# Value pages of the sampled sequences: key pages first, five buffers, the last value products inside the attention loop

## The chip, the cores and the metric

The kernel runs on one core of one Trainium2 chip. The metric is the device time of one execution in microseconds, the median over several executions. The core has five engines: TensorE (PE, matrix products), VectorE (DVE), ScalarE (ACT), GpSimd (POOL) and SyncE (SP), which here only issues transfers. ACT issues some transfers too, and POOL a few. All engines run their own instruction streams and meet at semaphores.

## What is computed

The reference is one inference step of a two-layer decoder for a prompt of 512 tokens and for 8 sampled sequences with one new token each. The even layer joins attention with a forgetting gate (8 heads of 64) and a convolution; the odd layer is a retention layer; each has a gated feed-forward part. The change touches the attention of the 8 sampled sequences over their paged past (1024 tokens, 8 pages of 128 tokens each, found through a page table):

```python
kp = cache_k[e, page_table].reshape(Bd, -1, H, hd)
vp = cache_v[e, page_table].reshape(Bd, -1, H, hd)
s_p = einsum('bqhd,bkhd->bhqk', q, kp) * scale
s_p = s_p + cq[..., None] - cum_p.transpose(0, 2, 1)[:, :, None, :]
p = softmax(concatenate([s_p, s_n], axis=-1), axis=-1)
o = einsum('bhqk,bkhd->bqhd', p[..., :P], vp) + einsum('bhqk,bkhd->bqhd', p[..., P:], v)
```

So 64 key pages and 64 value pages of 256 KB each are read, all of them once.

## The kernel before

The order of the work is written out by hand. After the input projection of the even layer comes the **attention loop**: 32 steps x = 0 to 31, a step for each of 8 heads and 4 blocks of 128 prompt queries. In each step PE transposes the weights of that step (line 715 in the rows), makes the scores of step x + 6 (L995 to L998) and, in every fourth step, a head's output (`head_out`, L1007). DVE finds the row maxima, ACT takes the exponentials and copies banks out, POOL divides by the row sums (L2443). The work of the sampled sequences, of the convolution and of the output projection is hung into the steps by tables at the top of the file (`V_AT`, `GATHER_AT`, `V_LOAD_AT`, `CONV_OUT_AT` and others).

**Key pages.** SP loads the 64 key pages into a ring of four buffers `kp`; page g may be loaded once POOL has made the product of page g - 4 (`key_pages`). POOL multiplies each page with a sequence's query row held in `QB` (three pages in a step, L2466), DVE sums the products (`dots`, L2019). POOL's stream is in order: the divisions and the products wait for one another.

**Value pages.** A *unit* u is four value pages; sequence b has the units 2b and 2b + 1. SP loads pages 0 to 2 of a unit and ACT page 3 (`values` and `V_LOAD_AT`), each through `value_unit` (from L619), which first waits until the buffer is free. Before the change the buffer is u modulo 3: `vp_a`, `vp_b`, `vp_c`. PE multiplies a sequence's eight pages with its weights (`past_values`, L1074, eight matmuls for each unit), ACT copies the bank into `vm`, which is the first two rows of `QB`, and PE picks each head's part out of it (`gather`, L1084), which DVE adds to `full_s` (L2081). The weights of sequences 0 to 3 are ready at step 16, those of 4 to 7 at step 26 (`DN_AT`).

Before, the value products of sequences 0 to 6 stand in steps 17, 19, 21, 23, 27, 29, 31. Those of sequence 7 and the gathers of 6 and 7 stand behind the loop (L1154 to L1156). SP's stream is in order too, and units 3 and 4 stand in it between key page 55 and key page 56.

**Output projection.** Its convolution half (`conv_out`, 24 matmuls each, line 827 in the rows) runs beside the loop in steps 19, 20, 22, 24, 25, 26, 28, 30, each with a weight block that ACT and DVE split into a high and a low part (`w_hi` L1360, `w_lo` L1802). Its attention half (`run("out_even", ...)`) runs behind the loop and starts with the gathered rows of the sampled sequences (`G_hi`, `G_lo`). PE fills steps up to 17 with idle products (L1121).

Of the kernel before, what the change touches and what calls it, by code (L numbers as in the profile page):

```python
# [17 lines left out]
D = 1024  # L18
# [3 lines left out]
NB = 8  # L22
# [6 lines left out]
NPG = NB * PAGES  # L29
# [62 lines left out]
EXP_AT = {15: 0, 25: 1}  # L92
DN_AT = {16: 0, 26: 1}

V_AT = {17: 0, 19: 1, 21: 2, 23: 3, 27: 4, 29: 5, 31: 6}
GATHER_AT = {18: 0, 20: 1, 22: 2, 24: 3, 28: 4, 30: 5}
V_LOAD_AT = {9: ((2, (0, 1)),), 10: ((2, (2, 3)),), 18: ((3, (3,)), (4, (3,))), 20: ((5, (3,)), (6, (3,))),
             22: ((7, (3,)), (8, (3,))), 24: ((9, (3,)), (10, (3,))), 28: ((11, (3,)), (12, (3,))),
             30: ((13, (3,)), (14, (3,)))}

PER_STEP = 3
STEP_PRODUCTS = 3
# [78 lines left out]
def psum_jobs():  # L181


    jobs = [(("xT", k), "D") for k in range(KD)] + [("xs", "D")]
# [22 lines left out]
    for h in range(HEADS):  # L207
        for q in range(TB):
# [25 lines left out]
            if x in DN_AT:  # L234
                jobs += [(("dn", DN_AT[x]), "D")]
            if x in GATHER_AT:
                jobs += [(("og", GATHER_AT[x]), "D")]
            if x in V_AT:
                jobs += [(("ov", V_AT[x]), "A")]
    jobs += [(("og", NB - 2), "D"), (("ov", NB - 1), "A"), (("og", NB - 1), "D")]  # L240
    for g in range(ADA_EVEN, ADA_LATE, 2):
        jobs += norm(1) if g == ADA_EVEN else norm(2) if g == ADA_NORM else []
        jobs += [(("adr", g), "A"), (("adr", g + 1), "A"), (("ada", g), "D"), (("ada", g + 1), "D")]
# [84 lines left out]
def build(nc, A):  # L328
# [3 lines left out]
    jobs = Jobs()  # L332
# [4 lines left out]
    def sb(name, shape, dtype=f32):  # L337
        t = nc.alloc_sbuf_tensor_at(name, shape, dtype, offset=at[0])
        at[0] += (math.prod(shape[1:]) * 4 + 31) // 32 * 32
        assert at[0] <= nc.sbuf_usable_end, (name, at[0])  # L340
        return t
# [90 lines left out]
    QB = sb("QB", [P, NB, 512])  # L432
# [13 lines left out]
    kp = sb("kp", [P, 4, 512])  # L446
# [11 lines left out]
    vp_c = sb("vp_c", [P, 4, 512])  # L458
    at[0] = ring_at
    vp_a = sb("vp_a", [P, 4, 2, 512])  # L460
    vp_b = sb("vp_b", [P, 4, 2, 512])
# [82 lines left out]
    with ctx:  # L544
        def sem(name):
            return ctx.enter_context(nc.semaphore(name))
# [6 lines left out]
        x_loaded, rows_loaded, pages_loaded = sem("x_loaded"), sem("rows_loaded"), sem("pages_loaded")  # L553
        raw_loaded = [sem(f"raw_loaded{i}") for i in range(4)]
        k_page = [sem(f"k_page{i}") for i in range(4)]
        v_unit = [sem(f"v_unit{i}") for i in range(3)]
        early_loaded = [sem(f"early_loaded{i}") for i in range(4)]
        spare_loaded = [sem(f"spare_loaded{i}") for i in range(4)]
        late_loaded = [sem(f"late_loaded{i}") for i in range(4)]
# [7 lines left out]
        sq_used, v_used = sem("sq_used"), sem("v_used")  # L567
# [23 lines left out]
        pad_ready, p_ready, prod_ready = sem("pad_ready"), sem("p_ready"), sem("prod_ready")  # L591
# [10 lines left out]
        cache_v = A["cache_v"][0].rearrange("n p h d -> n p (h d)")  # L602

        def page(eng, g, cache, dst, arrived):

            n = eng.value_load(pt_row[0:1, ds(g, 1)], min_val=0, max_val=cache.shape[0] - 1)
            eng.dma_start(dst, cache[ds(n, 1), :, :].rearrange("o p n -> p (o n)")).then_inc(arrived, 16)
# [6 lines left out]
            return (prod_a, prod_b)[g % 4 // 2][:, g % 2, :]  # L614

        def value_page(u, j):
            return vp_c[:, j] if u % 3 == 2 else (vp_a, vp_b)[u % 3][:, j, 1]

        def value_unit(eng, u, js):  # L619

            if u < 2:
                eng.wait_ge(block_done, N_OUT_EVEN)
                eng.wait_ge(lo_ready, N_OUT_EVEN)
            elif u == 2:
                wait_job(eng, ("cq", 1))
            elif u % 2 == 0:
                wait_job(eng, ("ov", (u - 3) // 2))
            else:
                eng.wait_ge(v_used, (u - 3) // 2 + 1)
            for j in js:  # L630
                page(eng, 4 * u + j, cache_v, value_page(u, j), v_unit[u % 3])

        def wait_job(eng, name):

            eng.wait_ge(job_done, jobs.done(name))
# [66 lines left out]
        def _(pe):  # L702
            def open_job(name):

                i = jobs.index[name]
                if i >= 4:
                    pe.wait_ge(emptied[jobs.engine[i - 4]], jobs.nth[i - 4])
                return Jp[i % 4]

            def close(mm):  # L710
                mm.then_inc(job_done, 1)
# [356 lines left out]
            def past_values(b):  # L1068
                bank = open_job(("ov", b))
                pe.wait_ge(samp_dve, 7 + 5 * (b // 4))  # L1070
                for u in (2 * b, 2 * b + 1):
                    pe.wait_ge(v_unit[u % 3], 64 * (u // 3 + 1))
                    for j in range(4):
                        mm = pe.matmul(bank[QD * j:QD * j + QD, :], weights_of(b, u % 2 * 4 + j), value_page(u, j),  # L1074
                                       start=u % 2 == 0, stop=u % 2 == 1)
                    if u % 2 == 0:
                        mm.then_inc(v_used, 1)
                close(mm)

            def gather(b):  # L1080
                bank = open_job(("og", b))
                wait_emptied(pe, ("ov", b))
                for t in range(4):
                    mm = pe.matmul(bank[:, 2 * t:2 * t + 2], vm[:, b % 2, t * P:(t + 1) * P],  # L1084
                                   con[:, C_OWN + 2 * t:C_OWN + 2 * t + 2], start=True, stop=True)
                close(mm)
# [23 lines left out]
            for h in range(HEADS):  # L1110
                for q in range(TB):
# [34 lines left out]
                    if x in DN_AT:  # L1146
                        past_total(DN_AT[x])
                    if x in GATHER_AT:
                        gather(GATHER_AT[x])
                    if x in V_AT:  # L1150
                        past_values(V_AT[x])
                    if x in CONV_OUT_AT:
                        conv_out(CONV_OUT_AT[x])
            gather(NB - 2)  # L1154
            past_values(NB - 1)
            gather(NB - 1)  # L1156

            pe.wait_ge(g_ready, 5)
# [197 lines left out]
        def _(act):  # L1356
# [112 lines left out]
            for m in range(20):  # L1469
# [22 lines left out]
                if m < 8 and m % 2 == 1:  # L1492
                    j = m // 2
# [5 lines left out]
                else:  # L1499
                    kind, j = m // 4, m % 4  # L1500
# [65 lines left out]
            def past_values(b):  # L1566
                wait_job(act, ("ov", b))
                if b >= 2:
                    wait_job(act, ("og", b - 2))
                n.up(f(vm[:, b % 2, :], Jp[jobs.bank(("ov", b))][:, :], ACT.Copy), emptied["A"])  # L1570
# [9 lines left out]
            for h in range(HEADS):  # L1580
# [3 lines left out]
                for q in range(TB):  # L1584
# [26 lines left out]
                    if x in EXP_AT:  # L1611
                        past_exps(EXP_AT[x])
                    if x in V_AT:
                        past_values(V_AT[x])
                    if x == SILU_AT:
# [6 lines left out]
                    if x in CONV_OUT_AT:  # L1622
                        ahead(N_OUT_EVEN + CONV_OUT_AT[x] + 2)
                    for u, js in V_LOAD_AT.get(x, ()):
                        if u == 2:
                            act.wait_ge(pages_loaded, 32)
                        value_unit(act, u, js)
            value_unit(act, 2 * NB - 1, (3,))
            past_values(NB - 1)

            def gates(layer):

# [149 lines left out]
        def _(dve):  # L1782
# [294 lines left out]
            def gather(b):  # L2077
                bank = bank_of(("og", b))
                for e in range(2):
                    r = slice(HD * e, HD * e + HD)  # L2080
                    o = v.tensor_tensor(full_s[r, 0:4, b], full_s[r, 0:4, b],  # L2081
                                        bank[r, 0:8].rearrange("p (t e) -> p t e", e=2)[:, :, e], ALU.add)
                n.up(o, emptied["D"])
# [26 lines left out]
            for h in range(HEADS):  # L2110
                for q in range(TB):
# [24 lines left out]
                    if x in DN_AT:  # L2136
                        past_scale(DN_AT[x])
                    if x in GATHER_AT:
                        gather(GATHER_AT[x])
                    for t in CONV_HI_AT.get(x - 1, ()):  # L2140
# [5 lines left out]
                    if x in CONV_OUT_AT:  # L2146
                        i = CONV_OUT_AT[x]
                        lo(N_OUT_EVEN + i + 2)
                        update(i, N_OUT_EVEN + i, mod_at(0, 2))
            gather(NB - 2)  # L2150
            gather(NB - 1)
            n.own(emptied["D"])
            step(v.tensor_copy(G_hi[:, 0:4, 0:NB], full_s[:, 0:4, :]))
# [374 lines left out]
        def _(sp):  # L2528
# [56 lines left out]
            def key_pages(first, end):  # L2585

                if first == 0:
                    for j in range(4):
                        page(sp, j, cache_k, kp[:, j], k_page[j])
                    return  # L2590
                with sp.Fori(first // 4, end // 4) as i:
                    for j in range(4):
                        sp.wait_ge(prod_ready, 4 * i + j - 3)
                        page(sp, 4 * i + j, cache_k, kp[:, j], k_page[j])

            def out_weights(first, end):

                for n in range(first, end):
                    half = 1 if n < N_OUT_EVEN + KD else 0
                    load_n(n, A["w_out_even"][0], 4 * half, P * ((n - N_OUT_EVEN) % KD), 4)  # L2600

            def values(first, end):
                for u in range(first, end):
                    value_unit(sp, u, (0, 1, 2, 3) if u < 2 else (0, 1, 2))

            N = N_OUT_EVEN
            key_pages(0, 4)
            out_weights(N, N + 4)
            values(0, 2)
            key_pages(4, 56)  # L2610
            values(3, 5)
            key_pages(56, 64)
            out_weights(N + 4, N + 6)
            values(5, 7)
            out_weights(N + 6, N + 7)
            values(7, 9)
            out_weights(N + 7, N + 9)
            values(9, 11)
            out_weights(N + 9, N + 11)
            values(11, 13)  # L2620
            out_weights(N + 11, N + 12)
            values(13, 16)
            out_weights(N + 12, N + 16)

            def ffn(layer):
                wg, wu, wd = A["w_ffn_gate"][layer], A["w_ffn_up"][layer], A["w_ffn_down"][layer]
# [102 lines left out]
```

## Time and profile before

| | us |
|---|---|
| median of 3 executions | 1847.53 |
| fastest and slowest of them | 1842.29, 1848.11 |
| the profiled execution, its own time | 1839.13 |
| span of its records, first to last instruction | 1837.3 |
| PE busy in the span | 1740.0 |
| DVE, ACT, POOL busy | 873.3, 579.0, 216.3 |

All times of the rows are microseconds from the start of the span. The attention loop's scores begin at 205.9 and its last head output ends at 384.1; the attention half of the output projection starts at 397.48. A busy engine in the profile is one that executes something, at whatever speed; the granted clock of PE stands in a column of its own (1.00 is full, 0.50 is half).

### The profile page before, as it was taken

What the parts mean: (1) busy time and instruction counts of PE and PEld (TensorE: products, weight loads), DVE (VectorE), ACT (ScalarE), POOL (GpSimd) and SP (SyncE); (2) the same over time, 40 slices, a digit from 0 to 9 for tenths busy, and PEclk for the clock granted to TensorE, in tenths of its full rate; (3) what the DMA queues carried; (4) which work ended last, traced back from release to release, by engine and by line L of the source; (5) the groups of instructions that cost most, each with busy time, mean ns of one, the idle gap of its engine ahead of it and who ended that gap; (6) DMA issues with size and microseconds to landing.
All of it is one profiled execution on the core that took longest, in us unless ns stands there. A gap on an engine that the chain in (4) does not pass through costs nothing.

```text
span 1837.3 us, 32367 instructions
## 1 busy us (share of the span) xinstructions
PE 1740.0 (95%) x13122; PEld 1556.5 (85%) x13122; DVE 873.3 (48%) x1529; ACT 579.0 (32%) x847; POOL 216.3 (12%) x229
## 2 busy tenths in 40 slices
PE   5899998988999999999999999999998999999998
PEld 3889754666999999998978888798687999999998
DVE  3599666626223233235417546365475533333335
ACT  2332344314321222223324434334323432222223
POOL 1000386202000000001001102001111000000001
PEclk7899998988999999999999999999999999999999
DMA  8554565674344535422324616237642233233321
GB/s 299 157 174 152 167 205 173 201 249 162 88 135 131 170 91 184 161 72 78 109 70 121 206 58 202 84 105 218 218 155 87 58 92 104 81 91 93 92 72 56
DMA packets 288329, 248.92 MB, mean 135 GB/s; under 512 B 9256, under 2 KB 240072, under 8 KB 288207
## 3 DMA queue, kind: packets, MB, share of 16 engines
q1 hardware_dynamic: 265156, 177.91, 32.1%
q0 software_dynamic: 15824, 58.99, 9.3%
q10 hardware_dynamic: 7235, 10.42, 1.7%
q8 instruction: 81, 1.33, 0.3%
q14 instruction: 33, 0.27, 0.1%
HBM read 224.05 MB, written 23.70 MB: 135 GB/s over the span
## 4 chain that ended last, share of the span: by engine, by line
PE 83%; DVE 6%; POOL 3%; ACT 3%; issue 3%; DMA 1%; ACTq 1%; SPq 0%; POOLq 0%; DVEq 0%
PE product L827 62%; PE product L842 5%; PE job L1327 2%; POOL sqa L2435 2%; PE job L721 2%; PE job L1310 1%; PE job L751 1%; PE job L715 1%; PE job L1302 1%; PE job L1201 1%; PE job L1221 1%; PE job L794 1%; PE job L1007 1%; DVE rstd L1832 1%; PE job L995 1%
## 5 line engine op out<-in xcount | busy, mean ns | idle before, releaser
L827 PE MATMUL product<-H_hi,w_lo 128*128 128x260 f32 x2368 | 676.4, 286 | 4.0 <-ACT gate L1360 3.7
L827 PE MATMUL product<-H_lo,w_hi 128*128 128x260 f32 x2368 | 671.0, 283 | 0.0
L827 PE MATMUL product<-H_hi,w_hi 128*128 128x260 f32 x2368 | 670.3, 283 | 0.0
L827 PEld LDWEIGHTS product<-H_hi,w_lo 128*128 128x128 f32 x2368 | 447.7, 189 | 17.4 <-issue 14.1
L827 PEld LDWEIGHTS product<-H_hi,w_hi 128*128 128x128 f32 x2368 | 448.4, 189 | 0.0
L827 PEld LDWEIGHTS product<-H_lo,w_hi 128*128 128x128 f32 x2368 | 448.0, 189 | 0.2
L1802 DVE TENSOR_TENSOR w_lo<-raw,w_hi 128x1024 fp32r<-128x1024 f32 (+2 forms) x244 | 279.8, 1147 | 160.0 <-ACT w_hi L1360 158.8
L1360 ACT ACTIVATE w_hi<-raw 128x1024 fp32r<-128x1024 f32 (+2 forms) x244 | 237.9, 982 | 209.6 <-PE product L827 155.9
L827 PE MATMUL product<-G_hi,w_lo 128*128 128x260 f32 x912 | 260.7, 286 | 6.1 <-DVE X L1887 2.5
L827 PE MATMUL product<-G_lo,w_hi 128*128 128x260 f32 x912 | 259.2, 284 | 0.0
L827 PE MATMUL product<-G_hi,w_hi 128*128 128x260 f32 x912 | 258.4, 283 | 0.0
L2187 DVE TENSOR_TENSOR full<-gate,product 128x520 f32<-128x520 f32 x44 | 30.7, 697 | 334.6 <-PE product L827 330.1
L827 PEld LDWEIGHTS product<-G_hi,w_lo 128*128 128x128 f32 x912 | 173.0, 190 | 11.6 <-issue 11.5
L827 PEld LDWEIGHTS product<-G_hi,w_hi 128*128 128x128 f32 x912 | 173.1, 190 | 0.0
L827 PEld LDWEIGHTS product<-G_lo,w_hi 128*128 128x128 f32 x912 | 172.9, 190 | 0.0
L1884 DVE TENSOR_TENSOR upd_s<-product,mod 128x8 f32<-128x8 f32 x80 | 13.3, 166 | 195.9 <-PE product L827 149.8
L1360 ACT ACTIVATE G_hi<-full 128x520 f32 (+1 forms) x44 | 28.2, 640 | 208.7 <-DVE full L2187 208.6
L1924 DVE SCALAR_TENSOR_TENSOR CV<-UP,vec,CV 128x512 f32<-128x512 f32 x120 | 80.9, 743 | 0.1
L1360 ACT ACTIVATE gate<-product 128x520 f32<-128x520 f32 x48 | 29.0, 605 | 156.2 <-PE product L827 156.1
L2435 POOL TENSOR_TENSOR sqa<-sq 128x520 f32<-128x520 f32 x5 | 6.5, 1298 | 559.6 <-ACT sq L1360 559.6
L2471 POOL DMA_DIRECT2D spare<-in_ada_w x24 | 18.0, 758 | 340.3 <-PE job L721 304.3
L842 PE MATMUL product<-G_hi,w_lo 128*128 128x260 f32 x176 | 50.2, 285 | 3.6 <-DVE w_lo L1802 3.6
(343 smaller groups left out, 2192.8 us busy)
## 6 DMA issues: line engine op xcount, KB each, us to landing
spare<-in_ada_w POOLq DMA_DIRECT2D x24, 1024.0 KB, 9.7
raw<-in_w_in_odd SPq DMA_DIRECT2D x48, 512.0 KB, 3.8
raw<-in_w_ffn_gate SPq DMA_DIRECT2D x44, 512.0 KB, 4.0
raw<-in_w_ffn_up SPq DMA_DIRECT2D x44, 512.0 KB, 3.7
kp<-in_cache_k SPq DMA_DIRECT2D x64, 256.0 KB, 2.9
raw<-in_w_ffn_down SPq DMA_DIRECT2D x32, 512.0 KB, 4.2
st<-in_state_ret POOLq DMA_DIRECT2D x28, 512.0 KB, 4.3
out_ret_sample<-st POOLq DMA_DIRECT2D x28, 512.0 KB, 4.8
```

The costliest lines, as they stand in the source:

```text
L715: return pe.transpose(out, src, ident[0:n, 0:n])
L721: mm = pe.matmul(bank[QD * q:QD * q + QD, :], cT[:, 4 * half + q, :], weights[:, q, :], start=half == 0, stop=half == 1)
L751: mm = pe.matmul(bank[:, j * 10:(j + 1) * 10], ada_rows(g)[:, j * P:(j + 1) * P], con[:, C_ALL:C_ALL + 10], start=True, stop=True)
L794: return pe.matmul(banks[c][:, 0:CH], con[:, C_MEAN:C_MEAN + 1].broadcast_to((P, P)), src[:, c * CH:(c + 1) * CH], **kw)
L827: mm = pe.matmul(Gp[slot][:, c, 0:CH], w[:, j, k, :], x[:, (first + k) % KD, cols], start=k == 0 and p == 0, stop=k == kt - 1 and p == 2)
L842: mm = pe.matmul(Gp[j][:, c, 0:CH], w[:, j, k, :], x[:, k, c * CH:(c + 1) * CH], start=k == 0 and p == 0, stop=k == kt - 1 and p == 2)
L1327: mm = pe.matmul(bank[:, j * P:L], RVN[:, j, e * P:(e + 1) * P], AD[:, j, 0:L - j * P], start=j == 0, stop=j == TB - 1)
L1360: return nc.scalar.activation(out, in_, func, **kw)
L1802: v.tensor_tensor(w_lo[:, j, 0:kt, :], raw[:, j, 0:kt, :], w_hi[:, j, 0:kt, :].bitcast(f32), ALU.subtract).then_inc(lo_ready, 1)
L1924: o = v.scalar_tensor_tensor(CV[:, t, NB:T], UP[:, t, w:w + L], cw, CV[:, t, NB:T], ALU.mult, ALU.add)
L2187: v.tensor_tensor(dst.rearrange("p (c n) -> p c n", c=2), up.rearrange("p (c n) -> p c n", c=2), Gp[1][:, :, 0:CH], ALU.mult).then_inc(slo ...
L2435: n.up(v.tensor_tensor(sqa[:], a, sq[:, k % 2, :], ALU.add), sq_used)
```

## The change

Six things change, and nothing else:

1. SP loads the key pages 4 to 63 in one go; units 3 and 4 come behind key page 63, not between pages 55 and 56.
2. The value products move: sequences 0 to 7 in steps 17, 20, 22, 24, 27, 28, 30, 31 (before 17, 19, 21, 23, 27, 29, 31 and behind the loop); the gathers of 0 to 6 in steps 19, 21, 23, 25, 28, 30, 31 (before 0 to 5 in 18, 20, 22, 24, 28, 30). Only the gather of sequence 7 stays behind the loop.
3. Units 11 and 13 get buffers of their own: the key ring `kp`, and rows 2 to 5 of `QB`, both free once all 64 key products are made. Units 12, 14 and 15 go to `vp_c`, `vp_a` and `vp_b`.
4. ACT issues page 3 of units 3 and 4 in step 18, of 5 and 6 in step 21, of 7 and 8 in step 23, of 9, 10, 11 and 13 in step 25, of 12 and 14 in step 28, of 15 in step 29.
5. SP's order behind it: units 9, 10, 11, 13, then two blocks of output weights, then 12, 14, 15, then the other five blocks.
6. The waits before a unit's loads follow the new buffers.

```diff
-V_AT = {17: 0, 19: 1, 21: 2, 23: 3, 27: 4, 29: 5, 31: 6}
-GATHER_AT = {18: 0, 20: 1, 22: 2, 24: 3, 28: 4, 30: 5}
-V_LOAD_AT = {9: ((2, (0, 1)),), 10: ((2, (2, 3)),), 18: ((3, (3,)), (4, (3,))), 20: ((5, (3,)), (6, (3,))),
-             22: ((7, (3,)), (8, (3,))), 24: ((9, (3,)), (10, (3,))), 28: ((11, (3,)), (12, (3,))),
-             30: ((13, (3,)), (14, (3,)))}
+V_AT = {17: 0, 20: 1, 22: 2, 24: 3, 27: 4, 28: 5, 30: 6, 31: 7}
+GATHER_AT = {19: 0, 21: 1, 23: 2, 25: 3, 28: 4, 30: 5, 31: 6}
+V_LOAD_AT = {9: ((2, (0, 1)),), 10: ((2, (2, 3)),), 18: ((3, (3,)), (4, (3,))), 21: ((5, (3,)), (6, (3,))),
+             23: ((7, (3,)), (8, (3,))), 25: ((9, (3,)), (10, (3,)), (11, (3,)), (13, (3,))),
+             28: ((12, (3,)), (14, (3,))), 29: ((15, (3,)),)}
+LATE_SLOT = {11: 3, 12: 2, 13: 4, 14: 0, 15: 1}
+def value_slot(u):
+    return LATE_SLOT.get(u, u % 3)
+def value_loads(u):
+    return sum(value_slot(i) == value_slot(u) for i in range(u + 1))
...
-    jobs += [(("og", NB - 2), "D"), (("ov", NB - 1), "A"), (("og", NB - 1), "D")]
+    jobs += [(("og", NB - 1), "D")]
...
         def value_page(u, j):
-            return vp_c[:, j] if u % 3 == 2 else (vp_a, vp_b)[u % 3][:, j, 1]
+            s = value_slot(u)
+            return (vp_a[:, j, 1], vp_b[:, j, 1], vp_c[:, j], kp[:, j], QB[:, 2 + j])[s]
...
             elif u == 2:
                 wait_job(eng, ("cq", 1))
+            elif u in (11, 13):
+                eng.wait_ge(prod_ready, NPG)
+            elif u == 12:
+                eng.wait_ge(v_used, 5)
+            elif u == 14:
+                wait_job(eng, ("ov", 4))
+            elif u == 15:
+                eng.wait_ge(v_used, 6)
             elif u % 2 == 0:
                 wait_job(eng, ("ov", (u - 3) // 2))
             else:
                 eng.wait_ge(v_used, (u - 3) // 2 + 1)
...
-            gather(NB - 2)
-            past_values(NB - 1)
             gather(NB - 1)
...
-            value_unit(act, 2 * NB - 1, (3,))
-            past_values(NB - 1)
...
-            key_pages(4, 56)
+            key_pages(4, 64)
             values(3, 5)
-            key_pages(56, 64)
             out_weights(N + 4, N + 6)
             values(5, 7)
             out_weights(N + 6, N + 7)
             values(7, 9)
             out_weights(N + 7, N + 9)
-            values(9, 11)
+            values(9, 12)
+            values(13, 14)
             out_weights(N + 9, N + 11)
-            values(11, 13)
-            out_weights(N + 11, N + 12)
-            values(13, 16)
-            out_weights(N + 12, N + 16)
+            values(12, 13)
+            values(14, 16)
+            out_weights(N + 11, N + 16)
```

## Rows read from the trace of the kernel before

**Rows 1.** The page: busy time of PE, and the chain that ended last, by engine.
```profile
PE 1740.0 (95%) x13122; PEld 1556.5 (85%) x13122; DVE 873.3 (48%) x1529; ACT 579.0 (32%) x847; POOL 216.3 (12%) x229
...
PE 83%; DVE 6%; POOL 3%; ACT 3%; issue 3%; DMA 1%; ACTq 1%; SPq 0%; POOLq 0%; DVEq 0%
```

**Rows 2.** Timeline of POOL: start, length, instruction, idle time before it and its releaser.
```profile
304.28 3.01 POOL L2466 TENSOR_TENSOR prod_b<-kp,QB 128x512 f32<-128x512 f32 x2
318.16 1.26 POOL L2466 TENSOR_TENSOR prod_a<-kp,QB 128x512 f32<-128x512 f32 x1 [10.87 <-DMA kp<-in_cache_k]
```

**Rows 3.** Timeline of SP's transfers, steps 17 to 20.
```profile
307.67 2.53 SPq L607 DMA_DIRECT2D vp_a<-in_cache_v  x3
310.97 2.53 SPq L607 DMA_DIRECT2D vp_b<-in_cache_v  x3
314.89 11.03 SPq L607 DMA_DIRECT2D kp<-in_cache_k  x8
```

**Rows 4.** Timeline of DVE, steps 18 and 19.
```profile
309.30 1.26 DVE L2019 TENSOR_REDUCE SC<-prod_b 128x8 f32<-128x512 f32 x2
319.45 0.69 DVE L2019 TENSOR_REDUCE SC<-prod_a 128x8 f32<-128x512 f32 x1 [8.89 <-POOL prod_a L2466]
...
320.41 3.19 DVE L1806 TENSOR_TENSOR G_lo<-CV,G_hi 128x520 fp32r<-128x520 f32 x2
323.52 2.38 DVE L1802 TENSOR_TENSOR w_lo<-raw,w_hi 128x512 fp32r<-128x512 f32 x2
```

**Rows 5.** Timeline of PE, steps 18 to 20: a gather, a head, value products, a transpose.
```profile
308.83 1.00 PE L1084 MATMUL job<-con,QB 128*128 128x2 f32 x8
...
312.93 4.03 PE L1007 MATMUL job<-PTS,VN 128*64 128x512 f32 x8 [1.61 <-ACT PTS L1360]
320.44 1.94 PE L1074 MATMUL job<-vp_c,SC 128*32 128x512 f32 x8 [3.47 <-DVE full_s L2081]
...
328.35 0.28 PE L715 MATMUL job<-con,SS_a 128*128 128x128 f32 x1
```

**Rows 6.** Busy time by stretch, then granted clock, DMA share, GB/s.
```profile
300.00:306.00 6.00, 6.00 (x14) 2.84 (x18) 4.41 (x9) 3.75 (x8) 2.92 (x4) 0.50 0.16 43
313.00:316.00 3.00, 3.00 (x5) 1.00 (x6) 0.00 (x0) 0.00 (x0) 0.00 (x0) 0.54 0.93 305
392.00:402.00 10.00, 8.04 (x37) 6.31 (x30) 1.30 (x5) 1.63 (x3) 3.12 (x4) 0.50 0.35 124
```

**Rows 7.** The chain that ended last, steps 20 and 21: start, length, what.
```profile
331.12 0.48 DVE nm L2008
...
332.41 4.35 DMA vp_c<-in_cache_v
...
336.81 1.10 PE job L1074 x8
...
340.01 2.99 PE product L827 x24
```

**Rows 8.** Value pages issued by ACT, 300 to 400 us: time from issue to landing.
```profile
DMA to landing us min/median/max: 3.7/4.1/4.4
```

**Rows 9.** Timeline of ACT: the page transfer that follows the one at 332.41.
```profile
333.48 0.35 ACTq L607 DMA_DIRECT2D vp_a<-in_cache_v  x1
```

**Rows 10.** The chain that ended last, step 31 and behind the loop.
```profile
381.75 2.34 PE job L1007 x8
384.09 1.07 PE job L1074 x8
...
388.09 3.61 DMA vp_a<-in_cache_v
...
393.75 0.60 ACT QB L1360
...
394.50 1.85 PE job L1084 x8
...
397.48 2.53 PE product L827 x10
```

More of the change, by code:

```diff
@@ L555, in build @@
         k_page = [sem(f"k_page{i}") for i in range(4)]
-        v_unit = [sem(f"v_unit{i}") for i in range(3)]
+        v_unit = [sem(f"v_unit{i}") for i in range(5)]
         early_loaded = [sem(f"early_loaded{i}") for i in range(4)]
@@ L630, in value_unit @@
             for j in js:
-                page(eng, 4 * u + j, cache_v, value_page(u, j), v_unit[u % 3])
+                page(eng, 4 * u + j, cache_v, value_page(u, j), v_unit[value_slot(u)])
         def wait_job(eng, name):
@@ L1071, in past_values @@
                 for u in (2 * b, 2 * b + 1):
-                    pe.wait_ge(v_unit[u % 3], 64 * (u // 3 + 1))
+                    pe.wait_ge(v_unit[value_slot(u)], 64 * value_loads(u))
                     for j in range(4):
@@ L2149, in _ @@
                         update(i, N_OUT_EVEN + i, mod_at(0, 2))
-            gather(NB - 2)
             gather(NB - 1)
```

## The prediction

> **What bounds the kernel now.** I read the page first. PE is busy for 1740 of 1837.3 us and holds 83% of the chain that ended last [rows 1], so only time that PE loses, or runs at half clock, can be won. Of the attention stage I then read the timelines of POOL, SP, DVE and PE, and the chain. Two places lose time.
>
> The first is a hole at steps 18 and 19. POOL finishes the product of key page 55 at 307.3 and stands idle for 10.87 us until page 56 lands [rows 2]. SP could not issue it: units 3 and 4 stand in front, unit 4 waits until sequence 0's products are done, and so the eight last key pages go out only from 314.89 [rows 3]. DVE needs page 56's product in step 18 and stands idle for 8.89 us at 319.45; behind it in its stream are the last two splits of the convolution (3.19) and the first two weight splits (2.38) [rows 4]. PE's value products of sequence 1 therefore start only at 320.44, 3.47 idle before them, and step 20 begins at 328.35 [rows 5].
>
> The second is the end of the loop. The last head is done at 384.09; then come sequence 6's products, a page that lands only at 391.7 (issue 388.09 and 3.61), sequence 7's products, a copy and a gather, and the output projection starts at 397.48 [rows 10]: 13.4 us. PE's clock has dropped to half by then (0.50 from 392 to 402 [rows 6]).
>
> **The change part by part.** I follow PE, in the span's time, from 316.96, where head 4 ends (312.93 and 4.03 [rows 5]). That head waits for ACT's copy of step 19's transposes, which doesn't move, so I keep it.
>
> *Key pages ahead.* Page 56 waits for products made long before, so it is there when POOL wants it at 307.3. DVE sums it at 310.56, directly behind 309.30 and 1.26, and its weight splits end at 325.90 - 8.89 = 317.0 [rows 4]. PE has sequence 0's gather behind the head now (1.00 [rows 5], moved from step 18), so it reaches the first `conv_out` at 318.0: PE is last, not DVE. With 2.99 for the block [rows 7], step 20 starts at 320.9 and not at 328.35: 7.4 earlier, but with sequence 1's products still to do.
>
> *Units 3 and 4 behind page 63.* Page 63 needs the product of page 59. POOL makes four products from 307.3 on, at 1.26 each [rows 2] with a division between, so about 313.9; unit 3 goes out by 318 and lands, at the 4.1 of a page [rows 8], at 322. PE reaches its second unit of sequence 1 at about 323. No wait, but a microsecond of cover only.
>
> *Products moved into the loop.* From 328.35 to 384.09 PE took 55.7 us with sequences 2 to 5 in it; now 1 to 6 lie there, two more, at two units of 1.10 each [rows 7]: +4.4. Gathers 1 to 5 lie there both times.
>
> *New waits at ACT's pages.* Before, ACT issued page 3 of unit 5 in step 20, behind that step's row maximum; from the maximum to the product it took 336.81 - 331.12 = 5.7 us, and a `conv_out` block of 2.99 on PE covered half of it [rows 7]. Now it issues in step 21, where no block follows. PE has only a gather, step 22's transposes and scores (together 340.01 - 337.91 = 2.1 [rows 7]) and the first unit (1.10): a wait of 5.7 - 3.2 = 2.5 in step 22. Unit 7's page is issued behind head 5 in step 23: about 0.8 for the issue (331.60 to 332.41) and 4.1 to land [rows 7, 8] against a gather, transposes, scores and a unit, some 3.9 (an estimate from the 2.1 and 1.10 above, with wider scores): a wait of 1.0 in step 24. Bounds for both together: zero if the pages land in time, 8.2 if each waits a whole landing. I take 3.5, because the rows for issue and landing are of the same instructions under the same load. The Trainium skill ("DMA: Bandwidth & Descriptors", section "Anatomy of one DMA") gives some 2.0 us fixed plus bytes over 436 GB/s, fitted on the software path; for 256 KB that is an estimate of 2.6, and the two waits would be 1.0 and 0. This trace has 4.1, and the measurement decides.
>
> *The other loads.* ACT issues four pages in step 25, 4 x 1.07 on its queue (332.41 to 333.48 is one [rows 7, 9]), with step 26's copy behind them; a `conv_out` block and a transpose cover that. If the cover were gone it would cost 4.3, less what PE still has to do. Units 9 to 15 go out one to three steps before use: nothing. The output weights behind unit 15 are the same number and wait for the same splits: nothing; without that cover, one landing of about 4.
>
> So head 7 ends at 320.9 + 55.7 + 4.4 + 3.5 = 384.5, 0.4 later than before: the loop's own win is spent on two more sequences.
>
> *The tail.* Behind head 7 stand sequence 6's gather (1.0), sequence 7's products (2.2), the copy (393.75 to 394.50, 0.8), the last gather at full clock (1.0, before 1.85) and 1.13 to the first product [rows 10]: 6.1, against 13.4. The projection starts at 390.6 instead of 397.48: 6.9 earlier.
>
> *The clock.* Before, the projection's first 4.4 us ran at half [rows 6]. With idle pieces of 0.8 and 1.1 only, shorter than the 1.61 in front of the drop at 313 [rows 5, 6], I expect full clock: -2.2. In return the wait of 2.5 in step 22 is longer than that 1.61, so I add one drop there, at the price of a head at either level, 4.03 - 2.34 = 1.7 [rows 5, 10]. Bounds of the clock terms: -2.2 to +3.4.
>
> **Sum:** -6.9 - 2.2 + 1.7 = -7.4 us. Everything behind is PE's chain and shifts as a whole. Against the profiled execution this is 1839.13 - 7.4 = 1831.7. That execution was 8.4 faster than the median shown, and the runs shown spread over 5.8; I subtract from the median: 1847.53 - 7.4 = 1840.1.
>
> **The rivals.**
> - *Full win.* The pages of steps 22 and 24 land in time and no clock drops there: -7.4 - 3.5 - 1.7 = -12.6, 1834.9. For it: if PE comes to step 22 later than I have it, each microsecond takes one off the wait, and the clock then stays up. Against it: no page of ACT's landed under 3.7 [rows 8]. Chance 0.22.
> - *Half a win.* The tail's clock drops as before, and step 24's wait drops it a second time: -7.4 + 2.2 + 1.7 = -3.5, 1844.0. For it: at 392 to 402 PE was busy for 8.04 of 10 us and still at 0.50, and in 300 to 306 busy throughout [rows 6]. Chance 0.22. Beside it, a rule of the Trainium skill ("TensorE: Matmul & The Clock Gate", section "HAM oscillation"): short compute between waits for transfers makes the clock fall at every such wait, which speaks against moving these products close behind their pages. In this trace the clock did fall at 313 behind a wait of 1.61, though that one was for ACT.
> - *Slower: each unit waits for its pages.* Place: steps 20, 22, 24 and 30, where pages are issued a step ahead. If each waits a whole landing (4.1) and drops the clock (1.7), that is 23.2 in place of the 5.2 in the sum: -7.4 + 18.0 = +10.6, 1858.1. It is slower by over 0.3% once waits and drops exceed 5.2 + 7.4 + 5.5 = 18.1. For it: unit 3 has a microsecond of cover. Against it: sequences 4 to 7 have their pages 5 us or more ahead. Chance 0.06.
> - *The hole stays.* POOL or DVE is held at step 18 by something else, and 7 us of hole stay: about -0.4, 1847.1. Against it: at 307.3 POOL waits for the page alone [rows 2]. Chance 0.05.
>
> **How the numbers follow.** My forecast has 0.45. A measurement of this kernel tells about 0.3%, 5.5 us, from no change. Faster by more: 0.45 x 0.9 for the forecast, 0.22 for the full win, a quarter of the half win: 0.68. Within 0.3%: 0.25. Slower: 0.07. The range reaches from the full win, with 3 us for the level of the runs, to the half win with 2: 1832 to 1846. It leaves out the last two rivals and some of the edges.
>
> **What would show it.** Right: POOL's idle time at page 56 is gone; step 20's first transpose comes about 7 us earlier; step 22 has a wait of some 2.5 us on `vp_c`; step 31's head ends near 384; behind it no wait for a page, and the projection starts near 390 at full clock. Wrong: head 7 ending much before 382 (the waits were overstated) or after 387; a new idle piece of POOL or DVE over 3 us in steps 18 to 24; PE at half clock behind 390; or a part behind the loop whose length changes.

## The result, and the profile after

| | before | changed |
|---|---|---|
| first comparison, median (runs) | 1842.29 (9) | 1832.56 (9) |
| fastest and slowest | 1838.85, 1848.11 | 1826.19, 1841.09 |
| ratio, 95% interval | | 0.9938 [0.9918, 0.9957] |
| the profiled execution, its span, mean granted clock | 1839.13, 1837.3, 0.975 | 1835.99, 1834.2, 0.971 |

The change is faster: by 9.7 us between the medians, by 11.4 (8 to 15) by the ratio. The forecast was 1840.1 and -7.4: right in sign, inside its range (1832 to 1846), 7.5 us too high. The changed kernel ran twice more beside the kernel before: ratios 0.9959 [0.9942, 0.9976] and 0.9940 [0.9920, 0.9961]. The mean of all 28 runs is 1834.0, that of 80 runs of the kernel before 1844.1: 10.1 us (standard error 1.0).

The two profiled executions differ by only 3 us, because one ran longer at half clock. The windows of the changed kernel, then of the one before (PE only: stretch, its length, PE's busy time and instructions, granted clock, DMA share, GB/s):

```profile
272.00:283.00 11.00, 10.46 (x44) 0.84 0.68 212
283.00:304.00 21.00, 21.00 (x60) 0.52 0.41 114
304.00:320.00 16.00, 12.33 (x63) 1.00 0.41 121
340.00:352.00 12.00, 9.94 (x49) 0.57 0.81 247
402.00:412.00 10.00, 10.00 (x73) 0.83 0.97 358
```

```profile
283.00:304.00 21.00, 18.47 (x82) 0.89 0.55 159
```

In steps that the change does not touch, PE was busy for all of 283 to 304 and had a clock of 0.52; before, the same stretch had 0.89. Everything behind stands some 8.4 us later in the record of the changed kernel for this reason (step 18's first transpose at 316.08, before at 307.66), so the rows below are compared by distances from that transpose.

**The hole at step 18 is closed.** POOL's timeline, then DVE's (start, length, instruction, idle before it and its releaser), to be held against [rows 2, 4]:

```profile
313.99 0.59 POOL L2460 TENSOR_SCALAR SS_b<-SS_b,ri 128x384 f32<-128x384 f32 x1 [1.78 <-DVE ri L2030]
314.54 3.01 POOL L2483 TENSOR_TENSOR prod_b<-kp,QB 128x512 f32<-128x512 f32 x2
317.51 1.73 POOL L2483 TENSOR_TENSOR prod_a<-kp,QB 128x512 f32<-128x512 f32 x1
```

```profile
318.30 1.25 DVE L2037 TENSOR_REDUCE SC<-prod_b 128x8 f32<-128x512 f32 x2
319.48 0.67 DVE L2037 TENSOR_REDUCE SC<-prod_a 128x8 f32<-128x512 f32 x1
320.07 3.32 DVE L1824 TENSOR_TENSOR G_lo<-CV,G_hi 128x520 fp32r<-128x520 f32 x2
323.31 2.38 DVE L1820 TENSOR_TENSOR w_lo<-raw,w_hi 128x512 fp32r<-128x512 f32 x2
```

Neither the 10.87 before page 56's product nor the 8.89 before its sum is left: both follow directly. SP's timeline shows the price, unit 3 behind the last key page:

```profile
305.92 19.78 SPq L620 DMA_DIRECT2D kp<-in_cache_k  x10
326.64 2.53 SPq L620 DMA_DIRECT2D vp_a<-in_cache_v  x3
329.95 2.54 SPq L620 DMA_DIRECT2D vp_b<-in_cache_v  x3
```

PE's timeline, steps 18 to 22 and from head 7 to the projection (see [rows 5, 10]):

```profile
316.08 0.55 PE L737 MATMUL job<-con,SS_a 128*128 128x128 f32 x3
...
321.93 4.50 PE L1029 MATMUL job<-PTS,VN 128*64 128x512 f32 x8 [3.06 <-ACT PTS L1380]
326.36 1.43 PE L1106 MATMUL job<-con,QB 128*128 128x2 f32 x8
...
330.60 0.27 PE L737 MATMUL job<-con,SS_a 128*128 128x128 f32 x1
...
332.07 1.10 PE L1096 MATMUL job<-vp_c,SC 128*32 128x512 f32 x8
332.98 1.05 PE L1096 MATMUL job<-vp_a,SC 128*32 128x512 f32 x8
...
340.79 1.94 PE L1096 MATMUL job<-vp_b,SC 128*32 128x512 f32 x8
344.79 1.95 PE L1096 MATMUL job<-vp_c,SC 128*32 128x512 f32 x8 [2.06 <-DMA vp_c<-in_cache_v]
...
392.80 2.34 PE L1029 MATMUL job<-PTS,VN 128*64 128x512 f32 x8 [0.78 <-ACT PTS L1380]
...
396.05 1.10 PE L1096 MATMUL job<-vp_a,SC 128*32 128x512 f32 x8
396.96 1.04 PE L1096 MATMUL job<-vp_b,SC 128*32 128x512 f32 x8
398.81 1.02 PE L1106 MATMUL job<-con,QB 128*128 128x2 f32 x8 [0.81 <-ACT QB L1380]
400.98 0.38 PE L849 MATMUL product<-G_hi,w_lo 128*128 128x260 f32 x1 [1.15 <-DVE G_lo L1824]
```

Step 20 begins 14.5 us behind step 18, before 20.7 (17.4 and 13.1 in the other two profiles of the changed kernel, 23.0 in the second of the kernel before). Sequence 1's products have no wait. Sequence 2's second unit, in step 22, has one of 2.06, and the two units there take nearly twice their time (1.94 and 1.95 against 1.10 and 1.05). The last step's head ends at 395.13 and the projection follows 5.85 us later, before 13.4; no page stands between. The chain of waits names step 22's page (start, length, what):

```profile
338.89 0.70 DVE nm L2026
...
340.31 4.43 DMA vp_c<-in_cache_v
...
344.79 1.07 PE job L1096
```

DVE's row maximum releases ACT, ACT issues, the page takes 4.43 us, and PE is there before it.

### The profile page after: what moved, and what is told of

The parts are those of the page before. It is cut to its first block, busy times and chain, and to the rows that moved or that the text cites. A ratio compares the mean times of both kernels' runs of the same rounds, so it can differ in the third digit from the quotient of the medians.

```text
span 1834.2 us, 32366 instructions
## 1 busy us (share of the span) xinstructions
PE 1741.2 (95%) x13122; PEld 1555.2 (85%) x13122; DVE 872.0 (48%) x1529; ACT 579.4 (32%) x847; POOL 216.5 (12%) x229
## 4 chain that ended last, share of the span: by engine, by line
PE 84%; DVE 6%; ACT 3%; POOL 2%; DMA 2%; issue 2%; ACTq 1%; POOLq 0%; DVEq 0%
PE product L849 62%; PE product L864 5%; PE job L1347 2%; POOL sqa L2452 2%; PE job L743 2%; PE job L1330 1%; PE job L737 1%; PE job L1029 1%; PE product L1143 1%; PE job L773 1%; PE job L1017 1%; PE job L1322 1%; DVE rstd L1850 1%; PE job L1221 1%; PE job L816 1%
## 5 line engine op out<-in xcount | busy, mean ns | idle before, releaser
L849 PEld LDWEIGHTS product<-H_hi,w_lo 128*128 128x128 f32 x2368 | 446.2, 188 | 17.5 <-issue 12.6
L849 PEld LDWEIGHTS product<-G_hi,w_lo 128*128 128x128 f32 x912 | 173.3, 190 | 13.4 <-issue 13.4
```

The costliest lines, as they stand in the source:

```text
L849: mm = pe.matmul(Gp[slot][:, c, 0:CH], w[:, j, k, :], x[:, (first + k) % KD, cols], start=k == 0 and p == 0, stop=k == kt - 1 and p == 2)
```

## The experiments

The kernels of one group ran beside the kernel before on one chip: the first four rows, the next four, the last three. The second and third groups hold the changed kernel again and are its second and third comparison. Mean clocks are of all runs of a row.

| kernel | median (runs) | ratio to the kernel before | mean clock |
|---|---|---|---|
| before, unchanged (c_before) | 1843.01 (12) | 0.9984 [0.9962, 1.0005] | 0.9709 |
| key pages ahead alone (e_keys) | 1843.72 (12) | 0.9993 [0.9975, 1.0012] | 0.9709 |
| the rest alone (e_loop) | 1842.38 (12) | 0.9997 [0.9978, 1.0016] | 0.9709 |
| changed, early pages (e_early) | 1831.79 (7) | 0.9935 [0.9907, 0.9963] | 0.9731 |
| changed, again (a_copy) | 1835.37 (12) | 0.9959 [0.9942, 0.9976] | 0.9736 |
| early pages, again (e_early2) | 1828.31 (6) | 0.9916 [0.9896, 0.9937] | 0.9765 |
| changed, SP issues all of units 3 and 4 (e_head) | 1834.32 (6) | 0.9942 [0.9924, 0.9960] | 0.9755 |
| early pages and e_head's edit (e_both) | 1832.34 (6) | 0.9935 [0.9915, 0.9954] | 0.9753 |
| changed, third time (a_copy2) | 1831.08 (7) | 0.9940 [0.9920, 0.9961] | 0.9743 |
| early pages, third time (e_early3) | 1826.40 (6) | 0.9911 [0.9894, 0.9928] | 0.9760 |
| early pages, ACT issues all of unit 3 (e_act) | 1829.95 (6) | 0.9921 [0.9901, 0.9942] | 0.9758 |

The medians of the kernel before beside them were 1845.15 (30 runs), 1842.86 (17) and 1844.65 (12).

**The kernel before, unchanged.**

> The kernel before, unchanged, once more, for the granted clock of each of its runs. Theory 1 (the spread of the runs is PE's clock): the time of a run falls by half of what its half-clock time falls, so span x (1 - mean clock) taken off each run leaves a nearly constant rest, 1791 us as in the profiled execution shown (1837.3 x 0.975), within 3 us, while the raw times spread over 5 to 12 us; the median comes out at 1842, not at the 1847.5 that my prediction subtracted from. Theory 2 (the spread has another cause): the rest spreads as much as the raw times.

Its runs went from 1836.45 to 1847.98, the thirty beside it from 1836.43 to 1855.69: the same program spreads over 19 us. PE's work takes up to twice as long at half clock (1.94 us against 1.10 for a unit), so a half-clock stretch in which PE works costs about half its length; span x (1 - mean clock) is that half for a whole run. With it taken off each run, the standard deviation of those twelve falls from 3.2 to 1.6 us, of the thirty from 4.9 to 2.9, of the seventeen from 3.5 to 2.6; of the last group's twelve it does not fall (2.7 and 2.9). Over all 71 it falls from 4.1 to 2.6: more than half of the variance goes with how long PE was granted half clock. What is left is less constant than theory 1 had it (1791 within 3 us): 1787 to 1792 in the twelve, 1785 to 1798 in all 71. The median was near 1844 in every group; the 1847.53 of three runs lay 2 to 5 us above it.

**One half of the change: the key pages alone.**

```diff
 # before.py
-            key_pages(4, 56)
+            key_pages(4, 64)
             values(3, 5)
-            key_pages(56, 64)
```

> The kernel before with the key pages 56 to 63 ahead of units 3 and 4 on SP, and nothing else. Theory 1 (my walk): the 8.89 us hole of DVE goes, but sequence 1's products in step 19 now wait for unit 3, which lands at about 322 in the span's time before, so the hole is traded for a wait of about 5 us and step 20 starts 0 to 2 us earlier than before: 0.999 to 1.0 of before. Theory 2 (the hole alone is the win): step 20 starts 7 us earlier and the kernel is 6 to 8 us faster, 0.996.

No gain (0.9993), as theory 1 has it. POOL's hole is gone here too (page 56's product directly behind the division, at 311.10), but PE's timeline shows what took its place:

```profile
317.85 1.10 PE L1074 MATMUL job<-vp_c,SC 128*32 128x512 f32 x8
322.71 1.10 PE L1074 MATMUL job<-vp_a,SC 128*32 128x512 f32 x8 [3.77 <-DMA vp_a<-in_cache_v]
...
328.24 0.27 PE L715 MATMUL job<-con,SS_a 128*128 128x128 f32 x1
```

Sequence 1's products still stand in step 19, and unit 3 is now the page that is late. Step 20 comes 19.63 us behind step 18's first transpose (308.61), 1.1 less than before. The hole had been hiding unit 3's landing.

**The other half: products and buffers moved, SP's old order of key pages.**

```diff
 # after.py
-            key_pages(4, 64)
+            key_pages(4, 56)
             values(3, 5)
+            key_pages(56, 64)
```

> The changed kernel with SP's old order at one place: units 3 and 4 between key pages 55 and 56. Theory 1: the hole of 9 to 11 us on POOL is back; sequence 1's products, which before ran inside that hole, stand behind it in step 20, so all that the tail wins (7.3 us) is spent in the loop: 0 to 2 us faster than before, 7 to 8 us slower than the changed kernel. Theory 2 (the moved products make the win, the key order little): 9 to 11 us faster than before, as the changed kernel.

No gain either (0.9997). The waits in 300 to 400 us, of POOL and then of PE (engine, line, what it waited for: us in total, times, longest):

```profile
POOL prod_a L2483 <- DMA kp<-in_cache_k: 11.2, 1, 11.2
```

```profile
PE product L849 <- issue: 6.9, 1, 6.9
...
PE job L1096 <- DMA vp_c<-in_cache_v: 2.3, 2, 1.8
```

The hole is back, now as 6.9 us of PE in front of the first `conv_out` (put down to "issue" in this view; DVE, which splits its weights, is late as before). The tail of this kernel is as short as in the changed one: from head 7's end (391.49 and 2.34) to the projection (399.67) 5.8 us. So the tail's win of 13.4 - 5.8 = 7.6 is paid back by two more sequences in the loop (4.4 by the prediction's rows) and waits for `vp_c` (2.3): 0.9 should be left, and 0.5 is what the ratio shows. **Neither half gains alone; together they gave 10 us**, since each pays for the other: the moved products give unit 3 time to land, and the key pages ahead pay for the moved products. The second half (moved products, new buffers, new load steps) was not split further.

**ACT's pages one step earlier.**

```diff
-V_LOAD_AT = {..., 21: ((5, (3,)), (6, (3,))), 23: ((7, (3,)), (8, (3,))), 25: (...),
+V_LOAD_AT = {..., 20: ((5, (3,)), (6, (3,))), 22: ((7, (3,)), (8, (3,))), 24: (...),
```

> The changed kernel with ACT's single pages issued one step earlier: units 5 and 6 in step 20 in place of 21, 7 and 8 in 22 in place of 23, 9, 10, 11 and 13 in 24 in place of 25. Theory 1: unit 5's last page lands before PE wants it, the 2.06 us wait of step 22 in the changed kernel's profile goes, and with it the clock drop behind it (1.94 in place of 1.10 for a unit and 5.03 in place of 2.98 for a block, 2.9 us): 3 to 5 us faster than the changed kernel, 14 to 16 faster than before, 0.992. Theory 2: another page or ACT's own copies come later by as much (the loads stand behind the copy of the value bank), and the time is that of the changed kernel, 0.994.

> The changed kernel once more, unaltered, beside the kernel before on one chip. In the first comparison it was 11.4 us faster (ratio 0.9938), but its mean granted clock was 0.975 against some 0.970 of the kernel before; with half of the half-clock time taken out of each run only about 4 us were left. Theory 1: the clock belongs to the change (two stops fewer: POOL's and DVE's hole, the page behind the loop); then the ratio is again 0.993 to 0.995 and the mean clock is again 0.003 to 0.005 above that of the kernel before. Theory 2: the clock was chance, the change itself gives what my sum has (-7.4) or less: ratio 0.996 to 0.998, mean clocks within 0.002.

> The kernel with ACT's pages one step earlier (V_LOAD_AT 21, 23, 25 to 20, 22, 24), in one call with the changed kernel. Theory: step 22's wait (2.06) and the half-clock stretch behind it (10.2 us at half, some 2.9 us) belong to that page; so this kernel is 2 to 5 us faster than the changed kernel beside it, and by the measure without the clock 3 to 4. Rival: the time of that wait comes back at the next due point (head 5 or 6 waits for ACT's copy, which is later by the two issues in front): then the two agree within 1 us by the measure without the clock.

> The changed kernel a third time, as the measure for the two kernels beside it. Theory 1 (the sum): ratio 0.994 to 0.997 of the kernel before, about -7.5 us as in the second comparison. Theory 2: the first comparison's -11.4 is the true size: ratio 0.993 or 0.994.

> The kernel with ACT's pages one step earlier, once more beside the changed kernel: by the two profiles its output projection starts 3.8 us earlier, and all behind it shifts as a whole. Theory: 3 to 5 us faster than the changed kernel beside it. Rival: what it gave in the last comparison (7 us) was half of it clock by chance, and the two earlier comparisons of different calls (0.9938 and 0.9935) are the truth: under 2 us.

The first result (0.9935) could not be told from the 0.9938 of another comparison, so both kernels ran side by side twice. There the early pages were 6.7 and 6.1 us faster by the means (1835.6 against 1828.9, 1833.8 against 1827.7), and 0.9916 and 0.9911 of the kernel before: a version that beats both. That is more than the 5 us expected at most. With span x (1 - clock) taken off, though, the gains are 1.1 and 2.9 us (standard errors 1.0 and 1.6), about the wait itself and less than the 3 to 4 expected by that measure; the larger part is clock. PE's waits in 300 to 400 us in the third group, the first two of the changed kernel and the whole list of the early pages:

```profile
PE job L1029 <- ACT PTS L1380: 4.1, 3, 2.5
PE job L1096 <- DMA vp_c<-in_cache_v: 2.8, 1, 2.8
```

```profile
PE job L1029 <- ACT PTS L1380: 4.0, 3, 2.5
PE job L1017 <- ACT PTS L1380: 2.5, 1, 2.5
PE job L1106 <- ACT QB L1380: 1.4, 2, 0.8
PE product L849 <- DVE G_lo L1824: 1.1, 1, 1.1
PE job L1017 <- DVE G_lo L1824: 0.2, 1, 0.2
```

All waits for pages are gone here (one of 0.5 in step 30 is left in the first profile of the early pages), and step 22's units (the timeline of the changed kernel, then of the early pages) show what went with them:

```profile
334.59 1.95 PE L1096 MATMUL job<-vp_c,SC 128*32 128x512 f32 x8 [2.76 <-DMA vp_c<-in_cache_v]
```

```profile
331.55 1.10 PE L1096 MATMUL job<-vp_c,SC 128*32 128x512 f32 x8
```

The windows of the same two (columns as above):

```profile
332.00:342.00 10.00, 7.41 (x38) 0.66 0.81 261
```

```profile
332.00:342.00 10.00, 9.76 (x62) 1.00 0.94 293
```

In the three profiles of the changed kernel step 22's waits were 2.06, 2.51 and 2.76 us, and half clock stood around or just behind each for 10.2, 3.4 and 6.8 us. In the three of the early pages there is no wait and no half clock at that place. So wait and half clock stand together three times and are gone together three times, and where they stand the step pays the 2.1 to 2.8 and half of the stretch wherever PE works in it. That the wait starts the stretch is shown less well. In the second and third profile the stretch begins behind the wait's end or inside it. In the first it begins ahead of it: the unit at 340.79, for which PE did not wait, already took 1.94 us, and the wait came behind that unit. And the second profile of the early pages has 3.4 us of half clock in step 24 with no wait over 0.3 us close ahead of it. The Trainium skill ("TensorE: Matmul & The Clock Gate", section "HAM oscillation") describes a kernel whose matmuls lose their clock at each wait for a transfer between them. Here the trace agrees in two of three profiles.

The stage, from PE's matmul number 1400 in order of start (at 214 to 216 us in every profile, ahead of all that is changed) to the projection's first, and the half-clock time in it:

| profile | stage | of it at half |
|---|---|---|
| before: two profiles | 183.3, 187.7 | 22.8, 34.0 |
| e_keys, e_loop | 186.2, 184.9 | 32.5, 31.2 |
| changed: three profiles | 186.6, 177.8, 176.8 | 44.4, 24.0, 20.5 |
| early pages: three | 174.6, 173.6, 170.9 | 17.3, 17.1, 13.9 |
| e_head, e_both, e_act | 182.5, 176.9, 169.9 | 23.9, 23.9, 13.7 |

From the second and third profile of the changed kernel to the early pages the stage shrinks by 4.3 us (177.3 to 173.0), more than the wait alone; the first is left out there, because 20.5 us of its half clock lie from 282.8 to 303.3, in steps that no kernel changes. With half of the half-clock time taken off, the stage is 171.9 and 170.7 before, 164.4, 165.8 and 166.6 in the changed kernel, 166.0, 165.1 and 164.0 with early pages: 5.7 us for the change by the means, 0.6 for the early pages.

Whether the clock is chance or belongs to the change is the question put down for a_copy. That comparison alone falls on the side of chance (0.9959, clocks 0.9736 and 0.9716), and the first, with 0.975, on the other. The third (0.9940, clocks 0.9743 and 0.9708) lies inside both theories' ratios. All runs together have a mean clock of 0.9742 for the changed kernel (28 runs, standard error 0.0005), 0.9707 for the kernel before (71 runs, 0.0003) and 0.9709 for either half. These runs come from different chips, and beside each other the clocks differ by 0.0020 and 0.0035 (standard errors 0.0009 and 0.0010). Both are more than two standard errors from zero, so a higher clock goes with the change, worth 3.7 to 6.4 us of a span of 1830; which of its parts brings it is not shown.

**Head 4's wait for ACT.** SP issues all four pages of units 3 and 4:

```diff
-V_LOAD_AT = {..., 18: ((3, (3,)), (4, (3,))), 21: ...
+V_LOAD_AT = {..., 21: ...
-                    value_unit(sp, u, (0, 1, 2, 3) if u < 2 else (0, 1, 2))
+                    value_unit(sp, u, (0, 1, 2, 3) if u < 2 or u in (3, 4) else (0, 1, 2))
```

> The changed kernel with page 3 of units 3 and 4 issued by SP behind the other three, and not by ACT in step 18. In the changed kernel head 4's products wait 3.06 us for ACT's copy of step 19's transposes, which stands behind ACT's two page issues (2 x 1.07 us with their waits). Theory: PE is the bound there, and the copy, head 4 and all behind it come 2.0 to 2.5 us earlier: 2 to 2.5 us faster than the changed kernel by the measure without the clock. Rival: SP's fourth page of unit 3 lands later than ACT's did, and sequence 1's products in step 20 wait for it instead: no difference (within 1 us), with a wait on DMA in front of step 20's products in the trace.

> Both edits together: ACT's pages of units 5 to 13 one step earlier, and page 3 of units 3 and 4 issued by SP. If the two waits are independent the gains add: 5 to 6.5 us faster than the changed kernel by the measure without the clock, and 0.990 to 0.992 of the kernel before. Rival: an earlier head 4 brings PE to step 20 and 22 before the pages of units 3 to 6 again, and part comes back as waits for pages: 3 to 4 us faster than the changed kernel, no better than the early pages alone.

PE's timeline of the first:

```profile
313.77 2.34 PE L1029 MATMUL job<-PTS,VN 128*64 128x512 f32 x8 [1.40 <-ACT PTS L1380]
...
326.08 1.95 PE L1096 MATMUL job<-vp_a,SC 128*32 128x512 f32 x8 [3.17 <-DMA vp_a<-in_cache_v]
...
340.69 1.10 PE L1096 MATMUL job<-vp_c,SC 128*32 128x512 f32 x8 [2.96 <-DMA vp_c<-in_cache_v]
```

The rival's wait came. The head's wait fell from 2.50 (a_copy) to 1.40, and sequence 1 now waits 3.17 for unit 3, whose fourth page SP issues last; its stage is 182.5. By the whole time it cannot be told from the changed kernel beside it (0.9942 and 0.9959, intervals overlapping); with the clock taken off it is 2.4 us slower (1789.5 and 1787.1, standard error 0.9), where the rival had no difference. With early pages as well (e_both) the gains did not add: 0.9935 against 0.9916 for the early pages alone, and two waits on `vp_c` are back, 2.3 us in total; with the clock taken off nothing is left of the 3 to 6.5 us that either theory gave it over the changed kernel (0.3 slower, standard error 0.7).

**Unit 3 on ACT, in the gap behind its copy.**

```diff
 # e_early, ACT's step
+                    if x == 19:
+                        value_unit(act, 3, (0, 1, 2, 3))
                     exps_at(x + AHEAD)
 # SP
-                    value_unit(sp, u, (0, 1, 2, 3) if u < 2 else (0, 1, 2))
+                    if u != 3:
+                        value_unit(sp, u, (0, 1, 2, 3) if u < 2 or u == 4 else (0, 1, 2))
```

> Early pages, and all four pages of unit 3 issued by ACT in step 19, between its copy of the transposes and the row sums (where it waits 3.59 us for DVE's row maximum), with unit 4 left to SP alone. Theory: head 4's wait for ACT's copy (2.50) falls to about 0.6, because no page issue stands in front of the copy, and unit 3 no longer waits in SP's queue behind the last key pages, where SP alone with four pages cost 3.2 us of wait: PE's output projection starts 1.5 to 2 us earlier than with the early pages alone, 5 to 6 us earlier than in the changed kernel; a gain this small is read from the trace. Rival: four issues (4.3 us) in ACT's idle 3.59 push its row sums and with them the copy of step 20's transposes, and PE loses there what it won: no gain over the early pages.

ACT's timeline shows the three late issues in what had been idle time:

```profile
311.82 0.60 ACT L1380 ACTIVATE PTS<-job 128x512 f32<-128x512 f32 x1
312.51 3.23 ACTq L620 DMA_DIRECT2D vp_a<-in_cache_v  x3
317.07 0.47 ACT L1380 ACTIVATE SS_a<-job,nm 128x256 f32<-128x256 f32 x1 [4.65 <-DVE nm L2028]
```

Head 4's wait falls to 1.40 (not to 0.6: two weight splits still stand in front of the copy), no page is late, and the stage is the shortest of all, 169.9. That is three microseconds below the mean of the early pages, of which only one is the wait. In whole runs it is not shown to be better (0.9921 and 0.9911, 6 runs each): inconclusive.

## Why the prediction was right or wrong

**Right: the mechanism.** Page 56 no longer stalls POOL and DVE. Unit 3 came with no wait. How thin that was shows in e_head, where a fourth page on SP made a wait of 3.17; with the products left in step 19 (e_keys) it is 3.77. The tail measured 5.85 where the working had 6.1 and the rows of before 13.4. Step 22's wait measured 2.06, 2.51 and 2.76 where 2.5 was forecast, in the place and on the buffer named. The Trainium skill's figures for a transfer ("DMA: Bandwidth & Descriptors", section "Anatomy of one DMA") had given, by an estimate, 2.6 us to a page and a wait of 1.0 to step 22. The page took 4.43, and the measurement decided.

**Slightly off.** Step 20 came 6.2 us earlier, not 7.4: in this profile head 4's start stands 5.85 behind step 18's first transpose (before 5.27), and the head and the gather ran at half clock longer (4.50 and 1.43 against 4.03 and 1.00). Step 24's wait of 1.0 did not come; one of 0.44 in step 30 came in its place (0.47 in the second profile; 0.6 in the third, put down to ACT). Counted from step 18 in the times of before, the last head ends at 386.7, 388.2 and 385.0 in the three profiles and the projection starts at 392.6, 394.1 and 390.9, where 384.5 and 390.6 were forecast. So the walk was 0.3 to 3.7 us short, and three of its own signs of being wrong are there: a head 7 behind 387 in one profile, half clock behind 390 in each, and new idle time of DVE, 5.3 to 5.8 us at step 22 (`w_lo` waiting for ACT's `w_hi`), which PE did not wait for.

**The steps that failed** are two.

1. *"I subtract from the median."* The text itself had noted that the runs shown spread over 5.8 us, and then took the level of three of them. Nine runs in the first comparison gave 1842.29, eighty gave a mean of 1844.1. From 1842.29 the same sum gives 1834.9, 2.3 from what was measured. That is 5.2 us of the 7.5 by which the forecast missed. Against all runs, which give 1834.0, it missed by 6.1: 3.4 for the level and 2.7 for the size.

2. *The clock terms*, -2.2 + 1.7 = -0.5. The mean clock rose by 0.0035 over all runs (0.0020 and 0.0035 beside each other); times a span of 1830 that is 6.4 us (3.7 and 6.4). The working let only the projection's first 4.4 us at half count. Around the wait behind the loop, half clock stood from 391.7 to 402.0 in the first profile of before, and for 10.2 and 13.7 us in c_before and e_keys; in e_loop and in all three of the changed kernel, where that wait is gone, it is 3.4 us at the projection's start. It did not go to zero, as was forecast ("I expect full clock"). The drop priced at 1.7 in step 22 was there each time, at half of 3.4 to 10.2 us where PE works. How the 10 us split between waits and clock is not exact. With span x (1 - clock) taken off, the change is 1790.23 - 1786.75 = 3.5 us (standard error 0.5); in the stage of the profiles it is 5.7. That measure counts half clock as loss even where PE only waited. So the mis-sized term is the clock's: 0.5 in the sum, 3.7 to 6.4 measured. The 6.9 of the other terms measured 3.5 to 5.7, and part of the error cancelled.

So the size, -7.4 against -10.1 measured, was short by the clock, and the forecast time was high by the level. In three comparisons the gain was 11.4, 7.6 and 11.1; the second has the sum inside its interval (4.4 to 10.7), the third only just at its edge (7.2 to 14.8), the first not (8 to 15). Where in the program the rest of the clock's gain lies stays open: seven profiles, four of kernels no faster than before and three of the changed one, differ by up to 20 us of half clock among themselves, and e_loop has the short tail without a higher mean clock (0.9709).

**The rivals.** "Half a win" (the clock in the tail drops as before) is out: 3.4 us at half against 10.2, and step 24 has no wait. "Slower" and "the hole stays" are out. "Full win", -12.6, needed step 22's page in time; it is what the early pages are: 15 and 16 us below the kernel before in the second and third comparison.

## What to carry to other kernels

A hole may be the cover of something else: before moving a stall away, ask which transfer or product lands inside it, and move that one too; here each half of the change alone gave nothing. A page that is needed in the step after its issue wanted one step more here, and a wait of 2 to 3 us on PE stood with a half-clock stretch that cost some 2 to 4 us on top (an estimate: half of the part of the 3.4 to 10.2 us in which PE worked). And take the level from as many runs as there are: the median of three runs of a kernel that spreads over 19 us lay 3.4 us above the mean of eighty.

## What was not expected of the hardware

Half clock also falls where PE waits for nothing. From 283 to 304 us PE was busy for all 21.00 us and had 0.52 (the first windows above), in steps that are the same in both kernels; PE's last idle time before was 0.54 us, ending at 282.25. The second and third profile of the changed kernel have full clock in most of it. Behind the projection's start, where all kernels run the same program, the rest, to the start of the last matmul, took 1428.8 us with 23.9 at half in the first profile of the changed kernel and 1439.3 with 41.0 at half in the third: 10.5 us between two executions of one kernel, for 17.1 us more at half. What starts such a stretch in a busy engine was not tried.
